# A hybrid decoder layer: gate and up products with seven products per tile, and a down product in a stage of its own

## The chip, the core and the metric

The kernel runs on one core of a Trainium2 chip. A core has a matrix engine (PE, or TensorE) with a queue for its weight loads (PEld), a vector engine (DVE), a scalar engine (ACT), a general one (POOL) and a queue engine (SP) that issues DMA transfers. ACT can issue transfers too. Each engine runs its own list of instructions in order, and engines wait for one another on semaphores. The metric is the device time of one execution in microseconds (us); lower is better.

## What is computed

One trunk layer on 1024 prompt tokens and 8 sample tokens, T = 1032 together. D_MODEL is 1024, D_FF is 2816. The change lies behind the mixing of the attention and memory branches:

```python
mixed = jax.nn.sigmoid(ga) * ya + jax.nn.sigmoid(gb) * yb
x = x + jnp.einsum('btd,de->bte', mixed, w_o)
h = _rmsnorm(x, norm2_g)            # x * rsqrt(mean(x*x) + eps) * norm2_g
ff = jax.nn.silu(jnp.einsum('btd,df->btf', h, w_gate)) * jnp.einsum('btd,df->btf', h, w_up)
return x + jnp.einsum('btf,fd->btd', ff, w_down)
```

## The kernel before

Activations lie feature by partition: a row block k is 128 features by 1032 tokens, 8 such blocks for D_MODEL. Every 32-bit number that goes through a product is held as a high part (rounded to fp32r) and a low part (the rest), and each product is three passes: high by high, high by low, low by high.

**Weights.** `weight_pieces` lists all weights in the order of their use, as pieces of 128x512. SP loads piece p into one of three slots `raw` (`load_weights`, L283); POOL makes the high part (L310) and the low part (L312) in a ring of 15 pieces `whi`, `wlo` (`split_weights`), and counts `w_lo`. PE counts `w_used` when a piece has served all its products. SP loads piece p when piece p - 3 has been split. Between pieces SP puts copies of 512 KB from cache to cache output (L288), as many as `copies_due` says; they have nothing to do with the products.

**Products.** `project_across` (L2163) makes one output tile, 128 features by 1032 tokens: for each row block k three passes, each of three matmuls over 344 tokens, into three PSUM banks. Two such groups of banks alternate.

**W_o product.** `Products.pe_third` makes 8 of these output tiles with 8 row blocks each. DVE adds each into `acc` (L2670), ACT squares it (L2634), DVE sums the squares (L2656). ACT and DVE make high and low parts of `acc` times the norm gain (L2504, L2661), the operand of the next stage. The norm's own factor, one per token, isn't in it.

**Gate, up and down.** `Ffn` goes through 11 pairs of feature tiles, j. For each it makes 4 output tiles (gate and up of both tiles, 8 row blocks each), then for the pair before 8 down tiles with 2 row blocks each, added into `acc` by DVE (L2884). DVE multiplies gate by the norm factor (L2858), ACT applies SiLU (L2837), DVE multiplies again (L2860) and by up (L2862), ACT and DVE make the high and low parts (L2841, L2864). The norm factor is made once, while the first gate product runs: PE sums the squares over partitions (L2794), ACT takes a root (L2832), DVE the reciprocal (L2873). At the end PE transposes `acc` (L2757), ACT and DVE copy it out, SP stores it.

## Time and profile before

| | us |
|---|---|
| median of 3 executions | 2204.04 (2201.41 to 2213.99) |
| span of the profiled execution | 2203.5 |
| PE busy | 2170.0 |
| PE weight loads busy | 2028.8 |
| DVE busy | 967.2 |
| POOL busy | 682.0 |
| ACT busy | 520.1 |

The span runs from the first to the last instruction of the one execution that was profiled. PE's busy time is how long at least one matmul was under way. The time of the executions and the span differ by half a microsecond, so a sum made against the span can be read as one against the median.

### The profile page before, as it was taken

Reading aid. Unit: us, or ns where it says so; the run is one execution under the profiler, and the core shown is the slowest. Engines: PE = TensorE matmul, PEld = TensorE weight load, DVE = VectorE, ACT = ScalarE, POOL = GpSimd, SP = SyncE. Lnnn points to the kernel's source line nnn. Section 1 sums busy time; section 2 is a strip of 40 time slices with the busy share of each in tenths; the row PEclk is TensorE's granted clock in tenths of the full one; section 3 lists DMA queues with packets and bytes.
Section 4 is the critical chain, followed back from the end, with each engine's and each line's share of the span. In section 5 each row is a group of like instructions: output and inputs, shape, how many; then the busy total and the mean of one; then the engine's idle time right before and its main releaser. Section 6 shows DMA issues by size and latency. Waiting matters only on the chain.

```text
span 2203.5 us, 33593 instructions
## 1 busy us (share of the span) xinstructions
PE 2170.0 (98%) x13518; PEld 2028.8 (92%) x13518; DVE 967.2 (44%) x1834; ACT 520.1 (24%) x1124; POOL 682.0 (31%) x654
## 2 busy tenths in 40 slices
PE   7999999999999999999999999999999999999998
PEld 6788899999877779999999999999999999999998
DVE  5675777774323422233375624353233332333324
ACT  5221455554333223344111101210000000000001
POOL 3432322132212222222333334454224432244310
PEclk9999999999999999999999999999999999999999
DMA  6634444355467736553576623444235432345402
GB/s 200 202 102 159 168 139 144 107 192 196 160 193 262 245 111 179 160 160 130 167 261 214 194 86 125 132 136 148 88 127 162 148 124 80 119 153 163 132 3 78
DMA packets 199642, 333.31 MB, mean 151 GB/s; under 512 B 39190, under 2 KB 111702, under 8 KB 196790
## 3 DMA queue, kind: packets, MB, share of 16 engines
q1 hardware_dynamic: 177454, 285.78, 40.3%
q10 hardware_dynamic: 22032, 45.38, 5.9%
q8 instruction: 107, 1.75, 0.3%
q14 instruction: 49, 0.40, 0.1%
HBM read 260.34 MB, written 158.83 MB: 190 GB/s over the span
## 4 chain that ended last, share of the span: by engine, by line
PE 56%; DVE 3%; DMA 1%; issue 1%; ACT 1%; SPq 0%; DVEq 0%; ACTq 0%
PE ps L2163 42%; PE ps L330 4%; PE ps L331 3%; PE ps L332 3%; PE ps L1601 1%; DMA h_mem<-c_ht 1%; PE ps L1376 0%; PE ps L1593 0%; PE ps L1584 0%; PE ps L1610 0%; DMA rw<-hm_t 0%; DVE misc L2873 0%; DVE x_a L2661 0%; PE ps L2757 0%; PE ps L1615 0%
## 5 line engine op out<-in xcount | busy, mean ns | idle before, releaser
L310 POOL CAST whi<-raw 128x512 fp32r<-128x512 f32 x316 | 241.3, 764 | 1397.6 <-PE ps L2163 564.2
L312 POOL TENSOR_TENSOR wlo<-raw,whi 128x512 fp32r<-128x512 f32 x319 | 441.0, 1383 | 38.7 <-issue 7.8
L2163 PE MATMUL ps<-x_a,whi 128*128 128x344 f32 x1656 | 307.8, 321 | 2.7 <-DVE misc L2858 1.8
L2163 PEld LDWEIGHTS ps<-x_a,whi 128*128 128x128 f32 x1656 | 269.2, 188 | 3.9 <-DVE misc L2858 2.1
L2163 PE MATMUL ps<-x_c,whi 128*128 128x344 f32 x1440 | 266.0, 320 | 3.1 <-DVE x_c L2509 1.9
L2163 PEld LDWEIGHTS ps<-x_c,whi 128*128 128x128 f32 x1440 | 233.3, 188 | 4.4 <-issue 4.4
L330 PE MATMUL ps<-whi,x_a 128*128 128x512 f32 x416 | 179.0, 430 | 0.0
L2163 PE MATMUL ps<-x_a,wlo 128*128 128x344 f32 x828 | 175.9, 321 | 0.0
L331 PE MATMUL ps<-wlo,x_a 128*128 128x512 f32 x416 | 167.1, 402 | 0.0
L332 PE MATMUL ps<-whi,x_a 128*128 128x512 f32 x416 | 167.0, 401 | 0.0
L330 PE MATMUL ps<-whi,x_b 128*128 128x512 f32 x416 | 166.0, 399 | 0.0
L332 PE MATMUL ps<-whi,x_b 128*128 128x512 f32 x416 | 166.0, 399 | 0.0
L331 PE MATMUL ps<-wlo,x_b 128*128 128x512 f32 x416 | 165.9, 399 | 0.0
L2884 DVE TENSOR_TENSOR acc<-acc,ps 128x1032 f32<-128x1032 f32 x88 | 107.9, 1228 | 117.8 <-PE ps L2163 117.8
L2163 PE MATMUL ps<-x_c,wlo 128*128 128x344 f32 x720 | 152.6, 320 | 0.0
L700 ACT ACTIVATE zt<-ps 128x512 f32<-128x512 f32 x104 | 62.1, 597 | 354.4 <-PE ps L332 303.6
L2163 PEld LDWEIGHTS ps<-x_a,wlo 128*128 128x128 f32 x828 | 140.1, 189 | 0.0
L2837 ACT ACTIVATE misc<-misc 128x1032 f32<-128x1032 f32 x22 | 23.5, 1067 | 425.0 <-DVE misc L2858 425.0
L2163 PEld LDWEIGHTS ps<-x_c,wlo 128*128 128x128 f32 x720 | 120.8, 188 | 0.0
L332 PEld LDWEIGHTS ps<-whi,x_a 128*128 128x128 f32 x416 | 104.3, 251 | 10.5
L2163 PE MATMUL ps<-rw,whi 128*128 128x344 f32 x528 | 113.0, 322 | 0.4 <-DVE acc L2884 0.2
L332 PEld LDWEIGHTS ps<-whi,x_b 128*128 128x128 f32 x416 | 103.5, 249 | 10.3
(349 smaller groups left out, 3795.8 us busy)
## 6 DMA issues: line engine op xcount, KB each, us to landing
out<-in_cache_kv_w SPq DMA_DIRECT2D x144, 512.0 KB, 5.2
raw<-in_w_in SPq DMA_DIRECT2D x147, 256.0 KB, 4.3
a_tr<-tt SPq DMA_DIRECT2D x48, 256.0 KB, 2.0
out<-in_cache_kv_w SPq DMA_DIRECT2D x24, 508.0 KB, 5.3
raw<-in_w_gate SPq DMA_DIRECT2D x88, 128.0 KB, 3.0
raw<-in_w_up SPq DMA_DIRECT2D x88, 128.0 KB, 3.8
raw<-in_w_down SPq DMA_DIRECT2D x44, 256.0 KB, 4.5
gates<-e_sg ACTq DMA_DIRECT2D x16, 516.0 KB, 4.1
```

Source lines behind the costliest of these rows:

```text
L310: pool.tensor_copy(self.whi[:, p % RING, :], raw).then_inc(self.w_hi, 1)
L312: pool.tensor_tensor(self.wlo[:, p % RING, :], raw, self.whi[:, p % RING, :].bitcast(F32), ALU.subtract).then_inc(self.w_lo, 1)
L330: nc.tensor.matmul(out, lhs[0], rhs[0], start=start, stop=False)
L331: nc.tensor.matmul(out, lhs[0], rhs[1], start=False, stop=False)
L332: return nc.tensor.matmul(out, lhs[1], rhs[0], start=False, stop=stop)
L700: act.activation(self.zt[:, u % Z, :], ps[:, u % 2, :], ACT.Copy, scale=self.scale(u)).then_inc(self.ev, 1)
L1601: last = pe.matmul(ps[:, bank, at], self.ww[:, self.at(h), :], self.v[:, b, h, :], start=True, stop=True)
L2163: last = nc.tensor.matmul(ps[0:m, bank + s, 0:SEG], w, x[:, s * SEG:(s + 1) * SEG], start=(k == 0 and i == 0), stop=(k == nk - 1 and i == 2))
L2837: act.activation(sg, sg, ACT.Silu).then_inc(self.sil, 1)
L2884: dve.tensor_tensor(seg3(acc[:, m, :]), seg3(acc[:, m, :]), self.res(x), ALU.add).then_inc(self.add, 1)
```

## The change

The gate and up products leave the list of pieces and get a path of their own. The operand h, normed in full now, is cut in four blocks: first or second half of the tokens (516 each), upper or lower four row blocks of features. Gate and up weights of one feature tile, upper and lower half, are the four blocks of the other matrix. Seven products of block sums (Strassen's scheme in Winograd's form) replace the eight. Each has 4 row blocks, 3 passes, 2 matmuls over 258 tokens: `across_half`. So DVE must make four sums of weights a tile, and once the sums of operand blocks. ACT rounds the weights, POOL makes the low parts, DVE puts the products together. The finished h tile goes to DRAM (`h_ff`). The W_o product is made by token halves, in the same form, so that the norm of the first half can be made while the second runs; its result goes to DRAM too (`x_mid`). After the last of 22 tiles the down product follows in four chunks of 6, 6, 6 and 4 tiles, with 8 output tiles a chunk, by `project_across` as before; h tiles and `x_mid` are loaded back.

```diff
+COPIES = (55, 121)
+MAKE = (1, 2, 4, 5, 6, 7, 3)
...
-    down = []
-    for j in range(DFF // 256):
-        out += [[(t["w_gate"][k * P:(k + 1) * P, j * 256:(j + 1) * 256], 0),
-                 (t["w_up"][k * P:(k + 1) * P, j * 256:(j + 1) * 256], 256)] for k in range(KD)]
-        out += down
...
+    for tiles in chunks_of():
+        out += [[(t["w_down"][e * P:(e + 1) * P, c:c + CW], 0)] for c in (0, CW) for e in tiles]
     return out
+def chunks_of():
+    return [range(0, 6), range(6, 12), range(12, 18), range(18, TILES)]
...
     def copies_due(self, p):
+        lead, first = 2 * KD, 13 * KD
+        if p < self.last:
+            return COPIES[0] * min(max(0, p + 1 - lead), first - lead) // (first - lead)
+        return COPIES[1] + (len(self.copies) - COPIES[1]) * (p + 1 - self.last) // DOWN
...
+    def pe_third(self, ffn):
+        for i in range(2 * KD):
+            g, half, m, u = self.third(i)
+            if i < 3:
+                pe.wait_ge(self.ev, 2 * KD)
+            else:
+                pe.wait_ge(self.oev, i - 2)
...
+                if i == 12 and k == 4:
+                    self.total(0)
...
+    def act_third(self, ffn):
+        for i in range(2 * KD):
+            square(i)
+            if i == 9:
+                for x in MAKE:
+                    ffn.act_round(0, x)
+            if i == 11:
+                ffn.act_root(0)
+            elif i == 12:
+                ffn.act_high(0)
+            elif i == 13:
+                ffn.act_high(1)
...
+            dve.tensor_tensor(half2(self.part(u, half)), half2(self.part(u, half)), self.pair(i), ALU.add).then_inc(self.oev, 1)
+            if i >= 1 and i != 12:
+                add_squares(i - 1)
+            if i == 9:
+                ffn.dve_sums(0, 0, 4)
+            if i == 11:
+                add_squares(11)
+                ffn.dve_var(0)
+            elif i == 12:
+                ffn.dve_inverse(0)
+                ffn.dve_scaled(0)
+            elif i == 13:
+                ffn.dve_scaled(1)
+                ffn.dve_low(0)
+            elif i == 14:
+                ffn.dve_low(1)
+                ffn.dve_across()
+        add_squares(2 * KD - 1)
...
+def across_half(core, bank, w, x, start, stop, again=False):
+    for i, (a, b) in enumerate(((w[0], x[0]), (w[0], x[1]), (w[1], x[0]))):
+        for s in range(2):
+            last = core.nc.tensor.matmul(core.ps[:, bank + s, 0:Q], a, b[:, s * Q:(s + 1) * Q], start=start and i == 0,
+                                         stop=stop and i == 2, skip_group_check=again)
...
+    def sequence(self, c):
+        return (1, 2, 5, 6, 7, 4, 3) if c == 0 else (1, 6, 7, 5, 2, 4, 3)
...
+    def dve_operands(self):
+        self.dve_var(1)
+        self.dve_inverse(1)
+        self.dve_scaled(2)
+        dve.wait_ge(core.w_used, core.last)
+        self.dve_minus(self.plain(5), self.block(2), self.block(0), [(self.yd, 8)])
+        self.dve_low(2)
+        self.dve_scaled(3)
+        self.dve_minus(self.plain(7), self.block(3), self.block(2), [(self.yd, 12)])
+        self.dve_minus(self.plain(6), self.plain(7), self.block(0), [(self.td, 8)], ALU.add)
+        self.dve_low(3)
+        self.dve_minus(self.plain(4), self.block(1), self.plain(7), [(self.td, 8)])
+        for at in (4, 5, 6):
+            self.dve_low(at)
...
+    def pe_product(self, c, x):
+        pe.wait_ge(core.a_lo, self.made(c, x))
+        if x == 2:
+            self.wait_taken(pe, c, "p1")
+        elif x == 4:
+            self.wait_sum(pe, c, "a")
+        elif x == 3:
+            self.wait_sum(pe, c, "c22")
...
+        for k in range(4):
+            if c == 0:
+                pe.wait_ge(self.tl, 4 * self.READY[x] + k + 1)
...
+    def sp_tile(self, c):
+        if c + 2 < TILES:
+            self.load(c + 2)
+        core.copy_until(COPIES[0] + (COPIES[1] - COPIES[0]) * (c + 1) // TILES)
+        if c == TILES - 1:
+            core.load_weights(core.last + 5)
+        self.wait_sum(sp, c, "ha")
+        sp.dma_start(core.h_ff[c, :, 0:HT], self.ha[a]).then_inc(self.h_out[a], 16)
+        if c == TILES - 1:
+            for e in range(10):
+                self.load_h(e)
...
+    def load_h(self, e):
+        if e < len(self.slots):
+            self.done(sp, TILES - 1, self.freed[slot])
+        else:
+            n = [e - len(self.slots) in tiles for tiles in self.chunks].index(True)
+            sp.wait_ge(core.w_used, self.piece(n, 4) + len(self.chunks[n]))
...
     def sp(self):
...
+        for k in range(KD):
+            sp.dma_start(self.acc[:, k, :], core.x_mid[k]).then_inc(self.products.x_in[k // 2], 16)
+        for n in range(len(self.chunks)):
+            last = self.piece(n, 4) + len(self.chunks[n])
+            core.load_weights(last - RAW)
+            if n + 2 < len(self.chunks):
+                for e in self.chunks[n + 2]:
+                    self.load_h(e)
+        core.load_weights(core.taken)
```

Where the order of instructions moves. Names behind "waits" are those of semaphore handles, which are used again in later stages, so only `w_lo` and `w_used` can be read as such. First SP, in the down product, at the passage from the first chunk to the second. Before, down pieces stood between those of gate and up:

```order
L288 DMA out<-in_cache_kv_w 16x8192
L283 DMA raw<-in_w_down 128x512 [waits w_lo]
L288 DMA out<-in_cache_kv_w 16x8192
L283 DMA raw<-in_w_gate 128x256 [waits w_lo]
L283 DMA raw<-in_w_up 128x256
L283 DMA raw<-in_w_gate 128x256 [waits w_lo]
```

Now, from the twelfth down piece (first row) on:

```order
L305 DMA raw<-in_w_down 128x512 [waits w_lo]
L313 DMA out<-in_cache_kv_w 16x8192
L3194 DMA rw<-h_ff 128x1032 [waits t_in0,w_used]
L3194 DMA rw<-h_ff 128x1032 [waits t_in1,w_used]
L3194 DMA x_a<-h_ff 128x1032 [waits t_in0,w_used]
L3194 DMA x_a<-h_ff 128x1032 [waits t_in1,w_used]
L3194 DMA x_c<-h_ff 128x1032 [waits t_in0,w_used]
L3194 DMA x_c<-h_ff 128x1032 [waits t_in1,w_used]
L305 DMA raw<-in_w_down 128x512 [waits w_lo]
L313 DMA out<-in_cache_kv_w 16x8192
```

Six loads of h tiles, which wait for `w_used` of the whole first chunk, now stand ahead of the thirteenth piece.

Second DVE, at the end of the W_o product. Before, from the last sum of squares to the first gate tile:

```order
L2656 TENSOR_TENSOR misc<-misc 128x1032 [waits a_std,a_var]
L2869 TENSOR_SCALAR misc<-ps 128x1024 [waits g_out,r_out]
L2871 TENSOR_SCALAR misc<-ps 128x8
L2873 RECIPROCAL misc<-misc 128x1032 [waits t_qk]
L2858 TENSOR_TENSOR misc<-misc,ps 128x1032 [waits g_w_in,dve_c]
```

Now, from the last half of `acc` (first row) on; the low parts of two more operands, 8 instructions, follow behind the last row:

```order
L2761 TENSOR_TENSOR acc<-acc,ps 128x516 [waits w_used]
...
L2990 RECIPROCAL misc<-misc 128x516 [waits g_out]
L3007 SCALAR_TENSOR_TENSOR acc<-acc,g,misc 128x516 [waits a_hs,a_xt,g_done]
...
L3061 TENSOR_TENSOR x_a<-x_a_f,x_a 128x516 [waits t_msk] x4
...
L3022 TENSOR_TENSOR x_c_f<-acc 128x516 [waits g_end] x4
L3022 TENSOR_TENSOR x_a_f<-x_c_f,acc 128x516 [waits t_qk] x4
L3061 TENSOR_TENSOR x_a<-x_a_f,x_a 128x516 [waits t_msk] x4
L3022 TENSOR_TENSOR acc<-acc,x_c_f 128x516 [waits t_qk] x4
L3061 TENSOR_TENSOR x_c<-x_c_f,x_c 128x516 [waits t_msk,t_qk]
```

Scaling, block sums and low parts of the operands now stand between the W_o product and the first tile of gate and up.

## Rows read from the trace of the kernel before

**Rows 1.** The page: busy us and share, then the chain's shares by line

```profile
PE 2170.0 (98%) x13518; PEld 2028.8 (92%) x13518; DVE 967.2 (44%) x1834; ACT 520.1 (24%) x1124; POOL 682.0 (31%) x654
...
PE ps L2163 42%; PE ps L330 4%; PE ps L331 3%; PE ps L332 3%; PE ps L1601 1%; DMA h_mem<-c_ht 1%; PE ps L1376 0%; PE ps L1593 0%; PE ps L1584 0%; PE ps L1610 0%; DMA rw<-hm_t 0%; DVE misc L2873 0%; DVE x_a L2661 0%; PE ps L2757 0%; PE ps L1615 0%
```

**Rows 2.** Windows: start:end, length, busy us (instructions) by engine, PEclk, DMA share, GB/s

```profile
1346.00:1437.00 91.00, 90.96 (x578) 90.71 (x577) 29.47 (x22) 17.15 (x16) 39.88 (x35) 1.00 0.46 158
1437.00:1461.00 24.00, 20.98 (x124) 19.23 (x123) 17.54 (x9) 4.93 (x5) 11.24 (x7) 1.00 0.43 140
1700.00:1800.00 100.00, 100.00 (x636) 100.00 (x635) 29.40 (x22) 7.47 (x7) 31.42 (x32) 1.00 0.29 95
```

**Rows 3.** Timeline of PE: start, length, line, tiles, shapes, count, [idle before]

```profile
817.21 0.39 PE L330 MATMUL ps<-whi,x_a 128*128 128x512 f32 x1
...
821.40 0.40 PE L330 MATMUL ps<-whi,x_b 128*128 128x512 f32 x1
```

**Rows 4.** Timeline of PE: narrow matmuls with full weights; sum over partitions

```profile
1101.15 1.10 PE L1376 MATMUL ps<-ct,pick 16*128 16x128 f32 x8
...
1448.33 1.88 PE L2794 MATMUL ps<-misc,ones 128*128 128x512 f32 x4
```

**Rows 5.** Timeline of PE around an idle stretch, then the window behind it

```profile
826.30 0.40 PE L646 MATMUL ps<-wlo,hs 128*40 128x512 f32 x1
829.17 0.50 PE L330 MATMUL ps<-x_a,whi 128*128 128x344 f32 x1 [2.47 <-PEq L1103]
829.47 0.49 PE L331 MATMUL ps<-x_a,whi 128*128 128x344 f32 x1
...
829.00:833.00 4.00, 3.83 (x15) 3.86 (x16) 2.28 (x3) 1.28 (x1) 0.00 (x0) 0.57 0.27 75
```

**Rows 6.** Timeline at the end of the product before W_o

```profile
1345.73 1.22 DVE L2614 TENSOR_TENSOR misc<-ps,rw 128x1032 f32<-128x1032 f32 x1
1346.99 1.62 DVE L2617 TENSOR_TENSOR acc<-acc,misc 128x1032 f32<-128x1032 f32 x1
```

**Rows 7.** Lines on DVE, ACT and POOL: count: duration ns min/median/max

```profile
L2656 DVE TENSOR_TENSOR misc<-misc x7: 1226/1226/2322, 1377.1 to 1443.8; 128x1032 f32<-128x1032 f32 x7
L2884 DVE TENSOR_TENSOR acc<-acc,ps x88: 1215/1229/1231, 1533.0 to 2194.8; 128x1032 f32<-128x1032 f32 x88
L312 POOL TENSOR_TENSOR wlo<-raw,whi x319: 1264/1292/2336, 6.0 to 2134.8; 128x512 fp32r<-128x512 f32 x160
```

**Rows 8.** Groups by line and shape: busy us, mean ns, idle before

```profile
L2873 DVE RECIPROCAL misc<-misc 128x1032 f32<-128x1032 f32 x1 | 6.6, 6603 | 1.1 <-ACT misc L2832 1.1
L2841 ACT ACTIVATE rw<-misc 128x1032 fp32r<-128x1032 f32 x22 | 23.5, 1068 | 220.2 <-DVE misc L2862 220.2
L310 POOL CAST whi<-raw 128x512 fp32r<-128x512 f32 x143 | 110.5, 773 | 520.4 <-PE ps L2163 504.7 <-DMA raw<-in_w_up 7.5 <-DMA raw<-in_w_down 5.8
```

**Rows 9.** Timeline of ACT's queue at the W_o product, and windows behind it

```profile
1348.72 4.05 ACTq L2603 DMA_DIRECT2D acc<-x_t  x8
...
1352.00:1354.00 2.00, 2.00 (x14) 2.00 (x13) 0.42 (x1) 0.00 (x0) 1.92 (x3) 1.00 1.00 376
1358.00:1360.00 2.00, 2.00 (x14) 2.00 (x13) 0.00 (x0) 0.00 (x0) 0.45 (x1) 1.00 1.00 377
```

**Rows 10.** The page: DMA issues, KB each, us from issue to landing; then window 1346:1370

```profile
raw<-in_w_o SPq DMA_DIRECT2D x16, 256.0 KB, 2.6
...
raw<-in_w_o SPq DMA_DIRECT2D x3, 256.0 KB, 6.6
```

**Rows 11.** Timeline of SP's queue, down pieces with a copy behind each

```profile
2072.79 2.26 SPq L283 DMA_DIRECT2D raw<-in_w_down  x2
...
2087.82 0.34 SPq L283 DMA_DIRECT2D raw<-in_w_down  x1
2088.20 0.52 SPq L288 DMA_DIRECT2D out<-in_cache_kv_w  x1
2089.75 0.34 SPq L283 DMA_DIRECT2D raw<-in_w_down  x1
```

More of the change, by code:

```diff
@@ L2680, in pe_third, with third, pair, part @@
-    def pe_third(self):
-        for u in range(KD):
-            self.product(2 * KD + u)
+    def third(self, i):
+        g, half, m = i // 8, i // 4 % 2, i % 4
+        return g, half, m, 4 * g + m
+    def pair(self, i):
+        j = 2 * (i % 3)
+        return self.core.ps[:, j:j + 2, 0:Q]
+    def part(self, u, half):
+        return self.acc[:, u, half * HT:(half + 1) * HT]
+    def third_complete(self, eng, i):
+        if i % 8 == 7:
+            eng.wait_ge(self.core.w_used, self.p0[2] + (i // 8 + 1) * KD)
+        else:
+            eng.wait_ge(self.omm, i + 1 - (i + 1) // 8)
@@ new lines, in total, with square @@
+    def total(self, half):
+        pe, core = self.core.nc.tensor, self.core
+        pe.wait_ge(self.sum, self.squares_before(2 * KD if half else 12))
+        for s in range(2):
+            at = half * HT + s * Q
+            last = pe.matmul(core.ps[:, 6 + s, 0:Q], core.ones[:], self.ssq[:, at:at + Q], start=True, stop=True)
+        last.then_inc(self.tot, 1)
+    def act_third(self, ffn):
+        act, acc = self.core.nc.scalar, self.acc
+        def square(i):
+            g, half, m, u = self.third(i)
+            cols = slice(half * HT, (half + 1) * HT)
+            act.wait_ge(self.oev, i + 1)
+            if i not in (0, 4):
+                act.wait_ge(self.sum, self.squares_before(i))
+            act.activation((self.ssq if i in (0, 4) else self.spare)[:, cols], self.part(u, half), ACT.Square).then_inc(self.sqd, 1)
+        act.wait_ge(self.prod, KD)
+        act.wait_ge(self.ev, 2 * KD)
+        for i in range(2 * KD):
[9 more added lines that the diff above has]
+                ffn.act_high(1)
@@ new lines, in plain, with dve_minus, dve_across @@
+    def plain(self, x):
+        return {1: self.block(0), 2: self.block(1), 3: self.block(3)}[x] if x < 4 else self.x32[x]
+    def dve_minus(self, out, one, two, order, op=ALU.subtract):
+        dve = self.core.nc.vector
+        for k in range(4):
+            for sem, value in order:
+                dve.wait_ge(sem, value + k + 1)
+            dve.tensor_tensor(out[:, k, :], one[:, k, :], two[:, k, :], op).then_inc(self.td, 1)
+    def dve_across(self):
+        self.dve_minus(self.block(1), self.block(1), self.block(0), [(self.tl, 4)])
@@ new lines, in act_high @@
+    def act_high(self, at):
+        act, core = self.core.nc.scalar, self.core
+        x = (1, 2, 5, 6, 7, 4, 3)[at]
+        if at == 0:
+            act.wait_ge(self.products.ev, 2 * KD)
+        elif at == 1:
+            act.wait_ge(self.products.sample.out, 16 * NB)
+        elif at == 2:
+            act.wait_ge(core.w_used, core.last)
+        for k in range(4):
+            if at < 2:
+                act.wait_ge(self.yd, 4 * at + k + 1)
+            elif x == 3:
+                act.wait_ge(self.yd, 12 + k + 1)
+            else:
+                act.wait_ge(self.td, {5: 4, 7: 8, 6: 12, 4: 16}[x] + k + 1)
+            act.activation(self.x[x][0][:, k, :], self.plain(x)[:, k, :], ACT.Copy).then_inc(self.th, 1)
@@ new lines, in pe @@
+        for c in range(TILES):
+            for x in self.sequence(c):
+                self.pe_product(c, x)
+                if c == 0 and x == 1:
+                    self.products.total(1)
+        for i, (n, m) in enumerate(self.order):
+            if i == 0:
+                self.wait_sum(pe, TILES - 1, "q")
+                self.wait_taken(pe, TILES - 1, "gate")
+            elif i == 1:
+                self.wait_sum(pe, TILES - 1, "c12")
+            else:
+                self.added(pe, i - 2)
+            tiles, p = self.chunks[n], self.piece(n, m)
+            waits = [(core.w_lo, p + 1)] if m % 4 == 0 else []
+            if m == 0:
+                waits.append((self.los[0], self.los[1] + tiles.start + 1))
+            last = project_across(core, len(tiles), p, slice(P * (m % 4), P * (m % 4) + P),
+                                  lambda k: self.h_operand(tiles.start + k), 3 * (m % 2), m % 4 == 3, waits)
+            if m % 4 < 3:
+                last.then_inc(self.mm[0], 1)
+            if n == len(self.chunks) - 1 and m:
@@ L2916, in _ @@
             products.sample.load_gates()
[L2917 removed]
+            core.load_weights(core.last)
+            products.sp_third(ffn)
             ffn.sp()
```

592 lines of the change are left out of this document (389 added, 203 removed).

## The prediction

> **What bounds the kernel now.** I read the page first: PE is busy for 2170.0 of 2203.5 us, and the chain that ends last runs mostly over PE, by L2163 above all [rows 1]. Then windows: in the W_o product PE idles 0.04 us of 91, inside gate, up and down not at all, and only 3.0 us between the two, from 1437 to 1461 [rows 2]. No other engine is busy for more than a third of these stretches. So from 1346 us on time is the number of matmuls times their distance, plus whatever wait the change brings. The distance: 636 matmuls of 344 tokens in 100 us, 157.2 ns each [rows 2].
>
> **Part 1, fewer matmuls.** Gate and up were 44 tiles x 8 blocks x 9 = 3168 matmuls of 344 tokens: 498.0 us. They become 22 x 7 x 4 x 6 = 3696 of 258 tokens. That width isn't in the trace. Its neighbours: 19 matmuls of 512 tokens start between 817.21 and 821.40, 232.8 ns apart [rows 3], and 344 tokens take 157.2. The line through both gives 118.5 at 258, plain proportion from 344 gives 117.9. The lower bound is what a full weight load permits: 8 matmuls of 128 tokens with 128 weight columns last 1.10 us, less about 0.3 for the tail of the last, 0.11 each [rows 4]. The upper one, if the 157.2 - 143.3 (344 at 2.4 GHz) = 13.9 ns were a fixed cost: 107.5 + 13.9 = 121.4. I take 118.0, which both neighbours support: 436.1 us, a gain of **61.9**. At the bounds gate and up gain 91 or 49. Down keeps its 1584 matmuls. W_o goes from 576 x 157.2 = 90.5 to 768 x 118.0 = 90.6: nothing (-5 or +3 at the bounds). Summing squares over partitions keeps its tokens: 1.88 us for 1024 [rows 4], now 0.9 for each half.
>
> The trace has 157.2 ns for 344 tokens. The Trainium skill (TensorE: Matmul & The Clock Gate, "Back-to-back issue gap") gives columns over 2.4 GHz plus about 2.5 ns, which is 145.8 for 344; the trace disagrees, by 8%. An estimate by that page for 258 is 110.0 ns, so 406.6 us for gate and up, 29 us less than I take.
>
> **Part 2, start of W_o.** PE's first three half tiles now wait for all 16 sums of the stage before. Before, DVE took the last tile from 1345.73 to 1348.61, and PE worked on the next tile meanwhile [rows 6], losing nothing to speak of [rows 2]. Now it stands for 2.9. Whether such a stop also halves the clock is open: after 2.47 us of idleness the next matmuls of 344 tokens started 0.30 us apart, which is the lower level (1.2 GHz), and over 4 us the clock was 0.57 on average [rows 5]. That cost up to 0.43 x 4 = 1.7 us of work; I count 1.5 where it happens. Here **+3.5** (2.5 to 4.5).
>
> **Part 3, start of gate and up.** The norm used to be applied to results, under cover of PE. Now seven operands must exist first, and DVE makes them. Prices: a DVE instruction with both inputs in SBUF takes 1.226 us for 1032 tokens undisturbed, 2.32 at worst when POOL works beside it [rows 7]; with PSUM as one input 1.229. Half: 0.62, between 0.54 (nothing fixed) and 0.95 (POOL always beside it); POOL is idle in most of this, so 0.62. An add from PSUM, with its fixed part exposed, 0.7. The reciprocal, half of 6.6: 3.3 [rows 8]. ACT's half, 0.55 to 0.6, runs behind DVE by one instruction. Let 0 be the end of the 12th half tile of W_o, when the first token half is complete.
> PE: four more half tiles of 5.66 and a sum over partitions of 0.9; ends at 23.6.
> DVE: norm factor ready at 10.6 (PE's sum 3.8, variance 0.7, root 0.6, the add of tile 13 at 6.6 in between, 3.3). Then to the last add 20 half instructions, 3 adds, 2 sums of squares: 15.8, so 26.4. The first gate product starts 2.9 late and takes 2.8, or 4.4 if the clock fell.
> Then PE's second sum ends at 31.7; variance, root, reciprocal 36.5. From here PE waits for DVE alone: 9 half instructions to the first block of product 5 (42.1), 16 to product 6 (52.0), 8 to product 7 (57.1). Product 4 waits for the sum "a", which stands behind the other 11 low parts, three weight sums and two adds: 16, at 67, and about 4 more as POOL begins the next tile's low parts beside it, 71. Products 4 and 3 end at 78.3, 4 with a fallen clock.
> So 54.7 us for work of 20.8 (7 products of 24 x 0.118, and 0.9): 33.9 lost, less the 3.0 lost today: **+31** (26 to 40, by 0.54 a half instruction, and by POOL disturbing more).
>
> **Part 4, the 21 other tiles.** A product takes 2.83 us and every wait has at least two products, 5.7 us, of slack: a bank is used again only after that. Per tile of 19.8 us DVE has 11 half instructions (7 us), ACT 7 roundings and 3 more (6), POOL 7 low parts of 1.29 (9 to 12) [rows 7]. DVE's sums for the next tile are queued between its adds, 0.6 to 2.3 us each; the slack covers them. I take 0, and put the other case among the rivals.
>
> **Part 5, start of down.** SP reaches the last tile at 0.8 us of it, puts three copies, then eight pieces with a copy behind each. Such pairs go at (2089.75 - 2072.79) / 7 = 2.42 us [rows 11]; the last is issued at 19.2, the tile ends at 19.8. Only then the store and loads of h go out, behind some 5 us of queued bytes. A tile of 528 KB takes 1.4 at 376 GB/s [rows 9]. First tile in at about 28.5, ACT 1.07 [rows 8], DVE 1.23: 31. The sixth is ready 7 later, at 38, and the first down tile ends at 39.4 instead of 19.8 + 8.5. Lost: 11, and 1 for the clock: **+12** (8 to 18). The rows of `x_mid` land by some 28 us after the tile's end, just in time for the third down tile.
>
> **Part 6, between chunks.** The six h loads wait until PE has finished chunk 1, and piece 13 stands behind them on SP. PE idles meanwhile: 6 x 1.4 = 8.4, the piece 2.6 from issue to landing [rows 10], POOL 2.0 (0.6 to 0.77 and 1.29) [rows 7, 8]: 13. Five more pieces at 2.42 and one copy more: 26.5, last block 1.4: 27.9 instead of 8.5, so 19.4. At the next passage four loads: 15.1. The last passage has no load ahead of it. **+34** (24 to 42). What hides it? Nothing: DVE and ACT wait for PE there.
> That a piece waits for transfers ahead of it, the trace shows in part: beside the eight loads of `acc` a piece took 6.6 us to land instead of 2.6 [rows 9, 10]. The Trainium skill (DMA: Bandwidth & Descriptors, "Queues, rings and completion order") says that each DMA engine takes a queue's descriptors in order. By that the piece stands behind all six; where it did not, the second rival's time holds.
>
> **Sum.** 2203.5 - 61.9 + 3.5 + 31 + 12 + 34 = 2222.1, and by the 0.5 us between span and median still **2222**, 0.8% slower.
>
> **Rivals.**
> (a) *Faster: the short matmul costs what the weight load allows.* With 111 ns for each of 4464 matmuls, gate and up take 410 and W_o 85: 31 us less, **2191**. For: 8 matmuls ran at 0.11 each [rows 4]. Against: two widths lie on a line through nearly zero [rows 2, 3]. Below 113.8 ns the change wins, below 111.4 by more than 0.5%. The 110.0 of the Trainium skill's page named above would be this case too.
> (b) *Transfers queued ahead delay a piece little.* Then each passage costs 1.9 + 2.6 + 12.1 + 1.4 + 1.4 - 8.5 = 10.9 at most, 13 us less in all: **2209**, no measurable change. Against: [rows 10].
> (c) *The 21 tiles are not free of waits.* 147 products with 0.2 us each at their starts: +29, **2251**. For: a start now comes every 2.83 us instead of every 11.3, and DVE, ACT and POOL share weights work. Against: 5.7 us of slack.
> (d) *It isn't the change it says.* If the built program still ran eight products, part 1 would be gone: 2284. Against: its list on PE holds 3696 + 768 = 4464 matmuls of 258 tokens in this form. 0.01.
>
> **Chances.** Forecast 0.55, with its own range 2211 to 2238. (a) 0.11. (b), or smaller stalls in parts 3 and 5, 0.17. (c) 0.16. (d) 0.01. A measurement of this kernel tells 0.5%, 11 us, from no change. Faster by more (under 2193): 0.11, of (a). Within: all of (b), and a tenth of the forecast's, 0.22. Slower: 0.67. The range reaches down to 2196, where most of (a) is left out, and up to 2248, where half of (c) is.
>
> **What would show it.** Right: matmuls of 258 tokens 118 ns apart in the middle tiles; PE idle about 30 us in the 55 after W_o's last half tile, waiting for DVE; windows at the two passages in the down product with PE idle 10 us in a row and DMA at 350 GB/s or more. Wrong: a distance of 111 or 122; idle PE inside the middle tiles; passages shorter than 10 us.

## The result and the profile after

| | before | after |
|---|---|---|
| median, us | 2205.46 (4 executions, 2201.41 to 2213.99) | 2243.94 (4 executions, 2239.33 to 2251.00) |
| ratio to before | | 1.0165, 95% interval 1.0134 to 1.0196 |
| span of the profiled execution, us | 2203.5 | 2244.7 |

The kernel became 1.65% slower; 0.8% slower was forecast, +18 us for what was +38.5 by the medians and +41.2 by the spans. The page of the changed kernel: busy times, the clock in 40 slices of 56 us, shares of the chain by line.

```profile
span 2244.7 us, 35954 instructions
PE 2138.5 (95%) x14240; PEld 1995.6 (89%) x14240; DVE 997.3 (44%) x2026; ACT 630.4 (28%) x1351; POOL 697.0 (31%) x632
...
PEclk9999999999999999999999999979999999898999
...
PE ps L2800 23%; PE ps L2194 16%; PE ps L361 4%; PE ps L362 3%; PE ps L363 3%; DMA raw<-in_w_down 2%; PE ps L1632 1%; DMA h_mem<-c_ht 1%; POOL wlo L338 0%; PE ps L1407 0%; DVE x_c L2544 0%; PE ps L1624 0%; DVE x_a L2544 0%; PE ps L1615 0%; PE ps L1641 0%
```

PE does 31.5 us less than in [rows 1] and is idle for 106 us instead of 33.5. `across_half` is L2800 now and `project_across` L2194. A transfer of `w_down` appears in the chain with 2%, where [rows 1] had none. The clock shows three dips.

Windows of the stretches that the prediction spoke of (start:end, length, busy us by engine with counts, PEclk, DMA share, GB/s):

```profile
1346.00:1354.00 8.00, 1.01 (x6) 0.73 (x5) 7.28 (x5) 0.66 (x2) 7.84 (x5) 0.67 0.28 77
1354.00:1362.00 8.00, 8.00 (x50) 8.00 (x50) 1.63 (x2) 0.47 (x1) 5.29 (x6) 0.69 0.94 339
1362.00:1450.00 88.00, 87.55 (x720) 87.22 (x720) 36.73 (x50) 20.19 (x32) 14.09 (x11) 1.00 0.22 81
1450.00:1506.00 56.00, 31.04 (x179) 30.04 (x178) 45.38 (x62) 19.32 (x32) 9.91 (x7) 0.73 0.24 75
1506.00:1930.00 424.00, 424.00 (x3519) 424.00 (x3519) 152.00 (x227) 115.93 (x203) 191.61 (x147) 1.00 0.47 160
```

They answer to [rows 2]. PE stands for 7 of the first 8 us, works with a clock of 0.69 for the next 8, loses 25 of the 56 us ahead of the second feature tile, and nothing in the 424 us of the 21 other tiles. Next the down stage: PE's row behind its stop at the start, PE's row behind its stop at the first passage between chunks, and what SP and POOL do with h tiles and weight pieces there:

```profile
1946.56 2.06 PE L2194 MATMUL ps<-rw,whi 128*128 128x344 f32 x6 [15.30 <-DVE rw L3329]
...
2029.27 2.06 PE L2194 MATMUL ps<-x_a,whi 128*128 128x344 f32 x6 [13.12 <-issue]
...
2016.18 0.80 SPq L3194 DMA_DIRECT2D rw<-h_ff  x2
2017.08 0.86 SPq L3194 DMA_DIRECT2D x_a<-h_ff  x2
2018.03 1.02 SPq L3194 DMA_DIRECT2D x_c<-h_ff  x2
2019.11 0.44 SPq L305 DMA_DIRECT2D raw<-in_w_down  x1
...
2027.21 0.61 POOL L336 CAST whi<-raw 128x512 fp32r<-128x512 f32 x1 [48.12 <-DMA raw<-in_w_down]
...
2016.00:2029.00 13.00, 0.15 (x1) 0.00 (x0) 1.23 (x1) 6.05 (x6) 1.71 (x2) 0.70 0.94 365
```

The piece is asked for at 2019.11, behind six loads of 516 KB, and POOL gets it at 2027.21, 8.1 us later, where 2.6 was the time of an unhindered one in [rows 10]. The DMA engines are 94% busy meanwhile, at 365 GB/s.

**Where the time went.** From the starts of the matmuls in both traces, in us:

| stretch | before | after | difference | forecast |
|---|---|---|---|---|
| to the end of the product before W_o | 1341.4 | 1346.2 | +4.8 | 0 |
| from there to the end of W_o | 91.1 | 104.2 | +13.1 | +3.5 |
| gate, up, down, output | 771.0 | 794.3 | +23.3 | +15.1 |

Gate, up and down can't be separated before, since down ran between them. After, they are 55.4 to the start of the second tile, 425.3 for 21 tiles, then a stop of 15.5 and 305.5 from the tiles' end to the last matmul of down, that stop included.

The first line can't be told from scatter. The code up to there is the same in the changed kernel and in the variants below, and in the profiled executions of these eleven kernels this point lies anywhere from 1340.2 to 1351.3. So spans are compared below by stretches, which repeat, where nothing was edited, within 0.6 us for W_o and within 2.6 us for the later ones, and times by their ratios.

### The profile page after: what moved, and what is told of

Its sections match the earlier page's. It is cut to its first block, busy times and chain, and to the rows that moved or that the text cites. A ratio compares the mean times of both kernels' runs of the same rounds, so it can differ in the third digit from the quotient of the medians.

```text
span 2244.7 us, 35954 instructions
## 1 busy us (share of the span) xinstructions
PE 2138.5 (95%) x14240; PEld 1995.6 (89%) x14240; DVE 997.3 (44%) x2026; ACT 630.4 (28%) x1351; POOL 697.0 (31%) x632
## 4 chain that ended last, share of the span: by engine, by line
PE 53%; DVE 4%; DMA 3%; issue 1%; POOL 1%; ACT 1%; SPq 0%; DVEq 0%; POOLq 0%; ACTq 0%
PE ps L2800 23%; PE ps L2194 16%; PE ps L361 4%; PE ps L362 3%; PE ps L363 3%; DMA raw<-in_w_down 2%; PE ps L1632 1%; DMA h_mem<-c_ht 1%; POOL wlo L338 0%; PE ps L1407 0%; DVE x_c L2544 0%; PE ps L1624 0%; DVE x_a L2544 0%; PE ps L1615 0%; PE ps L1641 0%
## 5 line engine op out<-in xcount | busy, mean ns | idle before, releaser
L336 POOL CAST whi<-raw 128x512 fp32r<-128x512 f32 x228 | 167.7, 735 | 1113.4 <-PE ps L677 432.1
L338 POOL TENSOR_TENSOR wlo<-raw,whi 128x512 fp32r<-128x512 f32 x231 | 320.1, 1386 | 32.8 <-issue 8.7
L2800 PE MATMUL ps<-x_a,whi 128*128 128x258 f32 x960 | 160.1, 290 | 19.3 <-DVE x_a L3061 12.3
L2194 PE MATMUL ps<-x_a,whi 128*128 128x344 f32 x792 | 150.6, 326 | 14.2 <-issue 13.1
L2800 PE MATMUL ps<-x_c,whi 128*128 128x258 f32 x960 | 155.3, 284 | 0.0
L2800 PEld LDWEIGHTS ps<-x_a,whi 128*128 128x128 f32 x960 | 137.4, 197 | 20.0 <-issue 12.8
L2194 PEld LDWEIGHTS ps<-x_a,whi 128*128 128x128 f32 x792 | 130.4, 192 | 15.8 <-issue 15.1
L2973 POOL TENSOR_TENSOR wlo<-wlo_f,whi 128x512 fp32r<-128x512 f32 x88 | 111.9, 1292 | 74.3 <-issue 70.4
L2800 PEld LDWEIGHTS ps<-x_c,whi 128*128 128x128 f32 x960 | 132.9, 191 | 0.1
L363 PEld LDWEIGHTS ps<-whi,x_b 128*128 128x128 f32 x416 | 103.6, 249 | 10.3
L362 PEld LDWEIGHTS ps<-wlo,x_a 128*128 128x128 f32 x416 | 105.4, 253 | 8.2
L362 PEld LDWEIGHTS ps<-wlo,x_b 128*128 128x128 f32 x416 | 103.5, 249 | 10.3
L361 PEld LDWEIGHTS ps<-whi,x_b 128*128 128x128 f32 x416 | 103.7, 249 | 10.0
```

What stands on the lines that cost most here:

```text
L336: pool.tensor_copy(self.whi[:, self.place(p), :], raw).then_inc(self.w_hi, 1)
L338: pool.tensor_tensor(self.wlo[:, self.place(p), :], raw, self.whi[:, self.place(p), :].bitcast(F32), ALU.subtract).then_inc(self.w_lo, 1)
L361: nc.tensor.matmul(out, lhs[0], rhs[0], start=start, stop=False)
L362: nc.tensor.matmul(out, lhs[0], rhs[1], start=False, stop=False)
L363: return nc.tensor.matmul(out, lhs[1], rhs[0], start=False, stop=stop)
L2194: last = nc.tensor.matmul(ps[0:m, bank + s, 0:SEG], w, x[:, s * SEG:(s + 1) * SEG], start=(k == 0 and i == 0), stop=(k == nk - 1 and i == 2))
```

## Experiments

Every variant starts from the changed kernel, whose ratio to before is 1.0165. Ratios compare a variant with the kernel before on the same chip.

| run | median, us | ratio | 95% interval |
|---|---|---|---|
| wait | 2239.16 | 1.0146 | 1.0122 to 1.0170 |
| worow | 2234.92 | 1.0119 | 1.0093 to 1.0144 |
| ffn | 2239.02 | 1.0136 | 1.0114 to 1.0157 |
| nolow | 2233.45 | 1.0129 | 1.0110 to 1.0147 |
| hload | 2239.96 | 1.0151 | 1.0130 to 1.0172 |
| down | 2237.79 | 1.0131 | 1.0105 to 1.0157 |
| pieces | 2210.02 | 1.0015 | 1.0004 to 1.0025 |
| cols64 | 2236.53 | 1.0133 | 1.0108 to 1.0157 |
| best | 2185.92 | 0.9903 | 0.9883 to 0.9923 |
| best2 | 2187.13 | 0.9911 | 0.9896 to 0.9926 |

The interval of one variant is some 5 us wide to either side, so for edits worth less than 10 us the stretch of the trace decides and the ratio only confirms.

### widths: the distance of matmuls by themselves

96 matmuls of each width behind one another, with 128, 64 and 32 weight columns, two operands and eight banks, nothing else running:

```diff
+for cols, widths in ((P, (512,) + WIDE), (64, NARROW), (32, NARROW)):
+    for width in widths:
+        for i in range(COUNT):
+            at = (i % 4) * P
+            last = pe.matmul(ps[0:cols, n % 8, 0:width], w[:, (i // 4) % 2, at:at + cols],
+                             x[:, i % 2, 0:width], start=True, stop=True)
+            n += 1
```

> Only matmuls, no part of the layer: 96 in a row of each width, with 128, then 64, then 32 weight columns, fp32r, operands in SBUF, nothing else running. Question: why do 258 tokens take 120.5 ns and not 118. Theory A (line): the matmul itself takes 0.457 ns a token at every width down to about 243, where the weight load's 111 ns takes over; then 258 reads 118 here, and the kernel adds 2.5 for another reason. Theory B (knee): the weight load, 111 ns, and the matmul are so near to each other that they disturb one another; then 258 reads about 120.5 with 128 weight columns and 118 with 64, while 344 and 512 stay at 157 and 235 with both. Theory C (fixed cost): columns over 2.4 GHz plus 13 ns at every width; then 258 reads 120.5, 344 156 and 512 226, with any number of weight columns.

Windows of that run, for 344 tokens, for 258 and 256, for 224 to 128, then with 64 columns for 258 and for 128 tokens:

```profile
91.00:105.00 14.00, 14.00 (x90) 14.00 (x90) 0.00 (x0) 0.00 (x0) 0.00 (x0) 1.00 0.01 1
156.00:178.00 22.00, 22.00 (x186) 22.00 (x185) 0.00 (x0) 0.00 (x0) 0.00 (x0) 1.00 0.00 1
201.00:243.00 42.00, 42.00 (x379) 42.00 (x378) 0.00 (x0) 0.00 (x0) 0.00 (x0) 1.00 0.01 1
...
281.00:291.00 10.00, 10.00 (x87) 10.00 (x86) 0.00 (x0) 0.00 (x0) 0.00 (x0) 1.00 0.01 2
311.00:316.00 5.00, 5.00 (x87) 5.00 (x85) 0.00 (x0) 0.00 (x0) 0.00 (x0) 1.00 0.02 3
```

A window also counts the two or three matmuls that its edges cut, so I take the distance from the first to the last start of each 96 (ns):

| tokens | 512 | 448 | 400 | 344 | 320 | 288 | 272 | 264 | 258 | 256 | 248 | 240 | 224 to 128 |
|---|---|---|---|---|---|---|---|---|---|---|---|---|---|
| 128 columns | 226.8 | 202.7 | 180.3 | 157.7 | 146.6 | 131.7 | 125.3 | 120.1 | 119.9 | 120.0 | 115.0 | 112.0 | 111.5 |

With 64 columns 512 tokens take 230.0, 344 take 156.0, 258 take 117.8, 192 take 88.6 and 128 take 60.0; with 32 columns 512 take 231.5 and the others nearly the same as with 64. So there is a floor of 111.5 ns, which falls when fewer columns are loaded. At 258 tokens the matmul lies 8 ns over the floor, and 2.1 ns over what it takes with half the columns. The Trainium skill (TensorE: Matmul & The Clock Gate, "LDWEIGHTS (loading the stationary operand)") gives columns over 1.2 for a load, by which an estimate is 106.7 ns for 128 columns and 53.3 for 64; the floors measured here are 4.8 and at most 6.7 ns above.

No theory holds as it stands. A fails at 258 tokens, 119.9 and not 118. B has both values of 258 nearly right, but 344 tokens gain almost as much from fewer columns (1.7 ns), and 512 take 227 and not 235. C has the three widths within 1.7 ns, but says that the columns don't matter. Whether B's disturbance is the reason for the 2.1 ns at 258 is therefore not shown.

### cols64: half the weight columns in the kernel

```diff
-            last = core.nc.tensor.matmul(core.ps[:, bank + s, 0:Q], a, ...
+            last = core.nc.tensor.matmul(core.ps[0:64, bank + s, 0:Q], a[:, 0:64], ...
```

> All 4464 matmuls of 258 tokens load 64 weight columns instead of 128, so half the output rows of W_o, gate and up are left as they were in PSUM; their number, tokens, operands, waits and order are unchanged. Theory (of the 120.5 ns between two of them, some 2.5 come from the load of 128 weight columns, which by itself takes 111.6 ns as the run of widths showed and is too near to the matmul's own time to be hidden whole): the distance becomes 118.0 and the time falls by 4464 x 2.5 ns = 11 us, to 2233, ratio 1.0115. Rival (in the kernel the 120.5 ns have another cause, such as the other engines' traffic or the operands' places): the distance stays at 120 to 121 and the time within 3 us of 2244.

The same window of the changed kernel and of cols64:

```profile
1520.00:1920.00 400.00, 400.00 (x3320) 400.00 (x3319) 143.52 (x215) 110.23 (x193) 179.24 (x136) 1.00 0.45 154
```

```profile
1520.00:1920.00 400.00, 400.00 (x3351) 400.00 (x3350) 144.25 (x215) 110.24 (x193) 181.95 (x139) 1.00 0.48 161
```

Over the 21 tiles the distance fell from 120.55 to 119.44 ns, in the middle of W_o from 121.0 to 119.6, and the time by 7 us (1.0165 to 1.0133). That is about half of what the theory wanted, and not the rival's nothing. Halving the columns that are loaded and written takes 1.1 to 1.4 ns off the 120.5. Why the kernel has 119.4 with 64 columns where bare matmuls have 117.8 isn't settled.

### wait and worow: the start of W_o

wait lets the first half tile start on 15 sums:

```diff
-                pe.wait_ge(self.ev, 2 * KD)
+                pe.wait_ge(self.ev, 2 * KD if i else 2 * KD - 1)
```

> The changed kernel; the first half tile of the W_o product waits for 15 sums of the stage before instead of 16, enough for its two PSUM banks. Theory (the wait for the last sum): PE's stop of 7.3 us ahead of the W_o product goes; the first half tile starts within 1 us, its last row block still waits for the low part of the last row, so it ends about 5 us earlier, and the clock doesn't fall: 5 to 7 us less than the changed kernel. Rival (the rows): the low parts of the rows hold the first half tile up anyway: under 1 us less.

The first half tile started at once, and PE stopped for 4.6 us at its last row block, in whose low part DVE was still late:

```profile
1354.97 0.87 PE L2800 MATMUL ps<-x_c,whi 128*128 128x258 f32 x4 [4.58 <-DVE x_c L2544]
```

From the end of the product before to the end of W_o it took 100.8 instead of 104.2 us, 3.4 less where 5 to 7 were expected, and the clock fell all the same (0.57 from 1355 to 1358). worow changes DVE's order and PE's:

```diff
             if u == 7:
-                for k in range(KD - 1):
+                for k in range(3):
                     self.rest(4 + KD + k, k, acc[:, k, :])
...
+        for k in range(3, KD):
+            self.rest(4 + KD + k, k, acc[:, k, :])
...
+        steps = [(i, range(0, 4)) for i in range(3)] + [(i, range(4, KD)) for i in range(3)]
...
```

> Only the start of the output product changes: VectorE evicts the last tile of the second stage as soon as it is complete and makes the low parts of rows 3 to 7 after it; TensorE takes rows 0 to 3 of half tiles 0, 1 and 2 first, then rows 4 to 7 of the three, and half tile 0 waits for 15 sums. Theory (the 7.3 us stop comes from what stands in VectorE's queue ahead of the eviction, and the operand's rows are late only one by one): the stop goes, no stop above 1.5 us is left among the first three half tiles, and the time falls by about 9 us from 2244, to 2235, so that the stage starts as the forecast wanted it. Rival (the low parts themselves, 1.8 us a row against 0.73 us in which TensorE uses one up, set the pace, whatever the order): the stop only moves behind row 3, as in the run with one sum fewer, and the time is 2239.

PE in worow, at the border of the two products, and where it first stops:

```profile
1342.24 0.63 PE L2194 MATMUL ps<-x_c,wlo 128*128 128x344 f32 x3
1342.71 0.64 PE L2802 MATMUL ps<-x_a,whi 128*128 128x258 f32 x4
...
1347.17 0.75 PE L2802 MATMUL ps<-x_a,whi 128*128 128x258 f32 x4 [2.11 <-DVE x_a L2544]
```

The stop of 7 us is gone. One of 2.1 us is left, above the 1.5 that the theory allowed, for the low part of row 3, which I had put behind the eviction. The stretch takes 98.3 us, 5.9 less than 104.2; the ratio gives 10 us, with 9 expected. The theory of DVE's order holds; by the stretch, which decides here, it expected 3 us too much.

### ffn and nolow: the start of gate and up

```diff
-                pe.wait_ge(self.products.oev, 2 * KD)
+                pe.wait_ge(self.products.oev, 2 * KD - 2 if x == 1 else 2 * KD)
...
-        for at in (4, 5, 6):
+        for at in (4, 5):
             self.dve_low(at)
+        self.dve_low(6, range(1))
...
+        if c == 0:
+            self.dve_low(6, range(1, 4))
+            self.dve_sums(1, 0, 3)
...
```

> Only the start of gate and up changes: the first product waits for 14 sums of the output product instead of 16 (its banks were freed by the fourteenth), and VectorE makes the first two sums of products of tile 0 ahead of the low parts of the last operand (three of four rows) and ahead of the weight sums of tile 1. Theory (what TensorE waits for there is VectorE's chain of some 35 us, one instruction behind the other, and the 10.4 us stop ahead of the fourth operand's product is the order of that queue): the first product follows the output product at once (2.8 us), the chain starts some 3 us earlier, the 10.4 us stop falls to 4 or 5 us; 8 to 9 us less, 2235.5. Rival (the weight sums of tile 1, now later, set the start of tile 1, or another engine does): TensorE stops in tile 1 instead and the time is 2241 or more.

```diff
+            w = HT if at < 2 else 8
-            dve.tensor_tensor(self.x[x][1][:, k, :], self.plain(x)[:, k, :], ...
+            dve.tensor_tensor(self.x[x][1][:, k, 0:w], self.plain(x)[:, k, 0:w], ...
...
-        hi, lo = self.x[x]
+        hi, lo = self.x[x] if x < 3 else (self.x[x][0], self.x[x][0])
```

> At the start of gate and up, the low parts of operands 5, 6, 7, 4 and 3 are made for 8 of 516 tokens only, and TensorE multiplies with the high part in their place, with the same number of matmuls in every tile (so the low-order part of the input of these five products is wrong; nothing else is left out). VectorE is spared 20 half-width instructions of 0.63 us, less about 0.1 us each that remain: 10.5 us undisturbed, and up to 3 us more where GpSimd disturbed the last eight of them. Theory (TensorE waits there for VectorE's chain, instruction by instruction): the stops before operands 5, 6 and 4 shrink from 8.2, 4.9 and 10.4 us to about 5.5, 2.5 and 6, 9 to 12 us less in all, 2233. Rival (the chain from the sum of squares over the root to ScalarE's high parts sets it, and the low parts are in its shadow): less than 4 us, 2240.

PE's stops in that stage: the changed kernel, then ffn, then nolow.

```profile
1453.03 0.72 PE L2800 MATMUL ps<-rw,whi 128*128 128x258 f32 x4 [2.49 <-issue]
1469.36 1.20 PE L2800 MATMUL ps<-x_a,whi 128*128 128x258 f32 x4 [7.89 <-DVE x_a L3061]
1479.29 1.20 PE L2800 MATMUL ps<-x_a,whi 128*128 128x258 f32 x4 [4.44 <-DVE x_a L3061]
1498.06 1.20 PE L2800 MATMUL ps<-acc_r,whi 128*128 128x258 f32 x4 [10.14 <-issue]
```

```profile
1456.61 1.14 PE L2714 MATMUL ps<-misc,ones 128*128 128x258 f32 x4 [1.72 <-DVE misc L2754]
1468.53 1.20 PE L2800 MATMUL ps<-x_a,whi 128*128 128x258 f32 x4 [7.88 <-DVE x_a L3061]
1478.47 1.20 PE L2800 MATMUL ps<-x_a,whi 128*128 128x258 f32 x4 [4.85 <-DVE x_a L3061]
1492.86 1.20 PE L2800 MATMUL ps<-acc_r,whi 128*128 128x258 f32 x4 [6.28 <-issue]
```

```profile
1463.15 1.20 PE L2800 MATMUL ps<-x_a,whi 128*128 128x258 f32 x4 [7.37 <-DVE x_a L3062]
1471.57 0.73 PE L2800 MATMUL ps<-x_a,whi 128*128 128x258 f32 x4 [2.91 <-DVE x_a L3062]
1483.16 1.20 PE L2800 MATMUL ps<-acc_r,whi 128*128 128x258 f32 x4 [4.05 <-issue]
```

From the end of W_o to the second tile: 55.4 us, 49.2 in ffn, 45.8 in nolow. ffn gave 6.2 where 8.5 was expected: the stop before the first product went, but PE then waited 1.7 us for the last sum of squares, and the stop before the product on `acc_r` shrank by 3.9 instead of 5 or 6. Of the rival's other place one trace is left: 0.4 us in the second tile. nolow gave 9.6 in this stretch, inside the 9 to 12 of the theory; its 21 tiles took 1.4 us more than the others', for no reason that I found. PE waits there for DVE's list, instruction by instruction.

### hload and down: the start of the down product

hload asks for eight h tiles inside the last tile of gate and up, down for six, and for four rows of `x_mid` ahead of the other h tiles; down also has the first two h tiles split ahead of the last two steps of that tile.

```diff
-            core.load_weights(core.last + 5)
+            core.load_weights(core.last + 1)
+            for e in range(8):
+                self.load_h(e)
+            core.load_weights(core.last + 5)
...
```

> The changed kernel; in the last gate and up tile SP issues eight h loads as soon as their slots are free, behind four of the eight down pieces, instead of all behind the eight pieces and the store of the last tile's first half. Theory (SP's order sets the start of down): the first down block starts 3 to 4 us after the last gate and up product instead of 15.6, the first tile isn't paced by loads: 12 to 13 us less. Rival (ACT and DVE): ACT and DVE reach the h tiles only behind the last tile's work and pace them at 1.2 us or more: 5 us less or fewer.

In hload the first stop was 5.5 us instead of 15.5, but a second one came, 5.06 us at 1957.68, and the stretch from the tiles' end to the end of down took 305.5 us, exactly as before the edit, where 12 to 13 less were expected. Behind the second stop lies a queue again and not the rival's pace of ACT and DVE. POOL's wait for a piece, SP's queue, and the add that PE then waited for:

```profile
1938.38 0.73 POOL L336 CAST whi<-raw 128x512 fp32r<-128x512 f32 x1 [10.70 <-DMA raw<-in_w_down]
...
1930.21 0.52 SPq L313 DMA_DIRECT2D out<-in_cache_kv_w  x1
1940.50 0.33 SPq L305 DMA_DIRECT2D raw<-in_w_down  x1
...
1951.03 4.12 SPq L3256 DMA_DIRECT2D acc<-x_mid  x8
...
1956.39 1.23 DVE L3349 TENSOR_TENSOR acc<-acc,ps 128x1032 f32<-128x1032 f32 x1 [17.76 <-DMA acc<-x_mid]
1957.68 2.08 PE L2194 MATMUL ps<-rw,whi 128*128 128x344 f32 x6 [5.06 <-DVE acc L3349]
```

SP stood 10 us ahead of the piece of 1940.50 until POOL had split an earlier one, which landed late behind the h loads (POOL had it at 1938.38), and the loads of `x_mid` went out at 1951.03 only. The stall had moved to the next thing in the same queue. down's edit of SP's list:

```diff
+            core.load_weights(core.last + 1)
+            for e in range(6):
+                self.load_h(e)
+            core.load_weights(core.last + 5)
         self.wait_sum(sp, c, "ha")
...
+            for k in range(4):
+                self.load_x(k)
         self.wait_sum(sp, c, "hb")
...
+        for e in range(6, 12):
+            self.load_h(e)
```

> Only the start of the down product changes: SyncE asks for the first 6 tiles of h inside the last tile of gate and up (one piece of w_down ahead of them), for four rows of x_mid next, then for the other tiles of h; ScalarE and VectorE split h tiles 0 and 1 ahead of the last two steps of the last tile. Theory (the 15.6 us stop is the order of SyncE's queue and of the splits, and the transfers fit beside the last tile): the stop falls below 2 us and no stop above 2 us follows in the first chunk; 13 to 15 us less, 2230. Rival (the DMA's rate of about 400 GB/s is the bound: some 5 MB have to land in this stretch): a second stop comes in the first tiles, as in the run with the earlier h loads, and the time is 2238 or more.

The stop at the start fell to 6.0 us, no second one above 2 us followed in the first chunk, and the stretch took 298.8 us: 6.7 less than 305.5, where 13 to 15 were expected. The 6 us that stayed come from the fourth piece, which waits on SP until the first is split and holds up the h loads behind it.

### pieces: the passages between chunks

```diff
             if n + 2 < len(self.chunks):
+                core.load_weights(last + len(self.chunks[n + 1]) - RAW)
                 for e in self.chunks[n + 2]:
                     self.load_h(e)
```

> The changed kernel; SP asks for the down pieces of the next chunk ahead of the h tiles of the chunk after it, at both passages. Theory (pieces queued behind h loads and behind SP's wait): both stops between chunks go, 18.0 and 16.3 us with the slow blocks behind them: 34 us less, about 2210. Rival (the operands): h tiles of the next chunk aren't rounded and split in time, or the transfers are at their limit anyway; then half or more of the two stops stays.

At the place where the changed kernel stood for 13 us, in a window of this run:

```profile
2005.00:2025.00 20.00, 20.00 (x129) 20.00 (x128) 3.61 (x3) 6.07 (x6) 3.72 (x4) 1.00 0.74 284
```

Both stops are gone. The down stretch takes 270.6 instead of 305.5 us, 34.9 less, and the ratio falls from 1.0165 to 1.0015, 33 us. One line that lets the weight pieces be asked for ahead of the h tiles is worth nearly all that the change lost.

### best and best2: the edits together

best has worow, ffn, down and pieces.

> The three other edits of this call together, and the down pieces asked for ahead of the h loads at the passages between chunks (34 us by its own run). Theory (each stop has a cause of its own, so that the gains add): 2244 - 34 - 9 - 8.5 - 13 = 2180, ratio 0.988 to the kernel before, faster than both. Rival (a common limit, the DMA's rate in the down stage or TensorE's clock, which rises late after each stop, takes part of it back): 2195 to 2205, no faster than before.

2185.92 us, 0.9903 of the time before, 1% faster than it and 58 us faster than the changed kernel. By the ratios the four edits bring 10 + 6 + 7.5 + 33 = 57, so they add up; the 2180 expected had counted 64.5 for them. The stretches: W_o 98.2 (from 104.2), to the second tile 49.4 (from 55.4), down 262.0 (from 305.5); together 55.5.

best2 asks for three pieces without copies between them, then for the h tiles, then for the rest:

```diff
-            core.load_weights(core.last + 1)
+            core.load_weights(None, core.last + RAW)
```

> The version with all four edits, and at the start of the down product SyncE asks for three pieces of w_down with no cache copy between them, then for h tiles 0 to 5, and only then for the other pieces and the copies. In the version before this, the fourth piece waited on SyncE for 5.8 us until GpSimd had split the first, which landed late behind four copies, and the h loads stood behind it. Theory (the remaining 5.2 us stop at the start of down is this place of SyncE's queue): the stop falls to under 1.5 us, 4 us less, 2182 and ratio 0.988. Rival (the copies that now come later, or the pieces behind them, are late for the first chunk): a stop of 4 us or more within the first chunk and no gain, 2186.

PE at the start of down in best:

```profile
1926.05 2.06 PE L2194 MATMUL ps<-rw,whi 128*128 128x344 f32 x6 [4.89 <-DVE rw L3352]
```

In best2 the first stop is 2.2 us instead of 5.0, but two of 0.6 and 0.8 us come 8 and 10.5 us later for lack of pieces, and the ratio is no better, 0.9911, where 0.988 was expected: the rival's outcome, though its stops are small. The stretch of down is 260.1, 1.9 us less, no more than such stretches scatter.

## Why the prediction was wrong in its size

**Part 1, the distance: the term was mis-sized.** I took 118.0 ns from a line through 344 and 512 tokens. It measured 120.55 over the 21 tiles, 425.3 us where 147 products at 118.0 make 416.3: 9.0 too little. The line was at fault: its point at 512 was 232.8 in [rows 3] and is 226.8 by itself, and the line through 157.7 and 226.8 gives 122.3 at 258, where bare matmuls take 119.9, so that two widths don't give the third. My upper bound of 121.4, a fixed cost, had the size: from 240 to 512 tokens the bare matmuls take 10.1 to 16.0 ns more than their tokens at 2.4 GHz, only a little less at the narrow end. As bare ones already take 119.9, what else goes on in the kernel costs at most 0.7 of the 2.5 ns. About half of the 2.5 goes with half the columns (cols64: 1.1 to 1.4 ns); the other half I could not place. Rival (a) went wrong there as well: its floor is real, 111.5 ns, but is reached only at 224 tokens. One small term ran the other way: 344 tokens take 158.0 and not 157.2 (a window counts the cut matmuls at its edges), so the 3168 matmuls that went away were worth 2.5 us more.

**Part 2, the start of W_o: the step that failed.** I read DVE's 1345.73 in [rows 6] as the moment when PE had finished, and so priced PE's wait at DVE's two instructions, 2.9 us. These are the rows just ahead of it in the trace of before, which I had not put beside it, with PE's last matmuls of one product and its first of the next:

```profile
1340.38 5.43 DVE L2509 TENSOR_TENSOR x_c<-acc,x_c 128x1032 fp32r<-128x1032 f32 x3
1345.73 1.22 DVE L2614 TENSOR_TENSOR misc<-ps,rw 128x1032 f32<-128x1032 f32 x1
...
1340.96 0.63 PE L2163 MATMUL ps<-x_c,wlo 128*128 128x344 f32 x3
1341.43 1.10 PE L2163 MATMUL ps<-x_a,whi 128*128 128x344 f32 x6
```

PE had gone on at 1341.43; the eviction was late by 4.3 us because three low parts of 1.8 us stood ahead of it on DVE. In the changed kernel everybody waits for that:

```profile
1345.14 5.40 DVE L2544 TENSOR_TENSOR x_c<-acc,x_c 128x1032 fp32r<-128x1032 f32 x3
...
1350.47 1.22 DVE L2649 TENSOR_TENSOR misc<-ps,rw 128x1032 f32<-128x1032 f32 x1
...
1351.72 1.59 DVE L2652 TENSOR_TENSOR acc<-acc,misc 128x1032 f32<-128x1032 f32 x1
...
1353.37 1.23 PE L2800 MATMUL ps<-x_a,whi 128*128 128x258 f32 x4 [6.99 <-DVE acc L2652]
```

Of the 9.6 us above the forecast, 4.3 are this. The clock is 1.9: the first half tile took 8.3 us instead of 5.8, and the +3.5 of the sum leaves only 0.6 for it beside the 2.9, though the text speaks of 1.5. The distance is 2.3 (768 matmuls at 121.0), less 0.5 for the 576 of before, which took 158.1. The first sum over partitions is 1.6; the prediction counted it as 0.9 and set it against the sum of before, which lies in the next stretch. worow, which changes DVE's order and PE's, gets 5.9 back.

**Part 3, the start of gate and up: right.** 54.7 us forecast, 55.4 measured, and nolow and ffn show the reason to be DVE's chain. It was no luck of the sum: counted from the end of the 12th half tile as in the prediction, products 5, 6, 7 and 4 began at 43.7, 53.7, 59.0 and 72.4, where 42.1, 52.0, 57.1 and 71 were forecast.

**Part 4, the 21 tiles: right.** Not one distance there is above 0.2 us; rival (c) did not happen.

**Part 5, the start of down: right in kind, 4.9 too small.** 15.5 us of stop and 1.4 of halved clock in the first tile make 16.9, not 12. I had let the first h tile land 8.7 us behind the last product and counted 5 us of queued bytes; ACT got it 13.0 behind it. SP had stood 5.5 us (1919.1 to 1924.7) for a slot of pieces, and asked for the eighth piece 2.6 us after the last product instead of 0.6 before.

**Part 6, between chunks: right.** 19.4 and 15.1 forecast; 18.0 and 16.3 measured (13.3 and 11.3 of stop, 4.7 and 5.0 more in the first tile behind). Of the 4.7, 2.6 are the lower clock, up to 2034.8; the other 2.1 are waits for POOL's low parts of pieces that still come one by one:

```profile
2036.68 1.21 PE L2194 MATMUL ps<-ff_lo,whi 128*128 128x344 f32 x6 [0.45 <-POOL wlo L338]
...
2038.60 1.23 PE L2194 MATMUL ps<-x_c,whi 128*128 128x344 f32 x6 [0.22 <-POOL wlo L338]
...
2040.92 1.22 PE L2194 MATMUL ps<-x_c,whi 128*128 128x344 f32 x6 [0.63 <-POOL wlo L338]
```

At the second passage they are 1.7 and 3.3. All of it goes when the pieces are asked for first, as pieces shows; rival (b) did not happen.

One reading at the head of the prediction was wrong, without effect on the sum: other engines were busy for more than a third of two of its stretches, POOL for 39.88 of 91 us and DVE for 17.54 of 24 [rows 2].

So of 22.6 us that the spans differ from the forecast, 4.8 arose ahead of the change, within the scatter, 9.6 the start of W_o, and 8.2 lie in gate, up and down: 9.0 distance, 0.7 and 4.9 at the two starts, less 2.5 for the distance before; the other 3.9 are a gain, 1 of them the first sum over partitions, now part of W_o, and 0.8 a shorter output after the last product (8.1 for 8.9 us); the rest I did not separate. The distance is thus the largest miss, 9.0 + 2.3 us, and the start of W_o the one where the path itself was read wrongly.

## What to carry to other kernels

A wait on a result is as long as everything that stands ahead of that result in its engine's list. Find when the producer's input was complete, in the consumer's own rows, and don't take the start of the producing instruction for it. When a stage is cut off from its neighbour, look at what each in-order queue still holds at the border: here one line of order in SP's list was worth 33 us, nearly the whole loss, and with three more such edits the algorithm with seven products won by 1%. And matmuls that load weights have a floor, here 111.5 ns for 128 columns: shrink a matmul only while it is well above it, and measure the distance at the very width instead of drawing a line to it.
